# Start addresses of the on-chip tiles: the work region at a multiple of 256 bytes, the raw tiles at a multiple of 64

## What is computed

```
def reference(x, ...):
    x = first_block(x, pre_norm_w, ..., w_out)         # hybrid_layer
    return second_block(x, ln_attn_pre_2, ..., ln_mlp_post_2)

def hybrid_layer(...):
    proj = rms_norm(x, pre_w) @ w_in                   # 1024 -> 6152 columns
    o_sb = merge_heads(stick_breaking_attention(q_sb, k_sb, v_sb)) * silu(sb_gate)      # 8 heads of 64
    o_g  = merge_heads(rms_norm(gated_delta_rule_chunked(...))) * silu(gdn_gate)        # 4 heads of 128
    merged = sigmoid(merge_sb) * (o_sb @ w_branch_sb) + sigmoid(merge_gdn) * (o_g @ w_branch_gdn)
    return x + rms_norm(merged @ w_out, post_w)

def second_block(...):
    x = x + rmsnorm(token_mixer(rmsnorm(x)) @ w_out)   # 4 differential and 8 forgetting heads
    u = square(relu(rmsnorm(x) @ w_up))                # 1024 -> 4096
    return x + rmsnorm(u @ w_down)                     # 4096 -> 1024
```

## The kernel before

| tiles | start, modulo 256 |
|---|---|
| `hT`, `ring`, `raw_ring`, `x1`, `sig_sb`, `consts` | 128 |
| `osb`, `ogd`, `mix`, `merged`, `ring_u`, `u`, `qk`, `b`, `sig_gd`, `rawb`, norm scratch, `wab_s`, `wf_s`, `cin` | 64 |
| `rawg`, `rawsb`, `g`, `s`, `diag`, `q_sq` | 112 |

## Time and profile before

### The profile page before, as it was taken

How to read it: one execution, slowest core, us unless ns; L and a number is a source line. 1 busy time by engine, 2 the same in 40 slices (tenths; PEclk the granted TensorE clock), 3 DMA queues, 4 the chain that set the end, 5 groups by cost and what they waited for, 6 DMA issues and landing times.

```text
span 1102.8 us, 15036 instructions
## 1 busy us (share of the span) xinstructions
PE 1088.4 (99%) x5749; PEld 889.9 (81%) x5749; DVE 537.1 (49%) x1155; ACT 570.2 (52%) x1086; POOL 436.1 (40%) x236
## 2 busy tenths in 40 slices
PE   8999999999999999999999999999999999999997
PEld 7877878778888788888778787789888888888886
DVE  3739789788665224142445455535111115444444
ACT  6556767767678642353465566554222224333333
POOL 4334342442433444543133322344444446444441
PEclk9999999999999999999999999999999999999999
DMA  9133121221322332623222321222333324322212
GB/s 261 48 91 87 48 68 41 76 59 37 97 58 60 93 96 96 229 78 80 77 66 70 97 77 59 77 88 75 107 95 96 96 96 134 105 97 96 97 47 77
DMA packets 140530, 97.24 MB, mean 88 GB/s; under 512 B 9014, under 2 KB 125091, under 8 KB 140459
## 3 DMA queue, kind: packets, MB, share of 16 engines
q1 hardware_dynamic: 138728, 95.03, 29.0%
q10 hardware_dynamic: 1730, 1.25, 0.4%
HBM read 94.14 MB, written 2.91 MB: 88 GB/s over the span
## 4 chain that ended last, share of the span: by engine, by line
PE 95%; ACT 2%; DVE 1%; DMA 1%; issue 0%; POOL 0%; SPq 0%; ACTq 0%; DVEq 0%
PE bank L460 32%; PE bank L1191 14%; PE bank L1173 14%; PE bank L489 6%; PE bank L845 4%; PE bank L871 4%; PE bank L855 4%; PE bank L1204 2%; PE bank L667 1%; PE bank L685 1%; PE bank L610 1%; PE bank L598 1%; PE bank L1019 1%; PE bank L981 1%; PE bank L1001 1%; PE bank L1008 1%
## 5 line engine op out<-in xcount | busy, mean ns | idle before, releaser
L2457 POOL TENSOR_TENSOR ring<-raw_ring,ring 128x1024 fp32r<-128x1024 f32 x160 | 389.7, 2439 | 574.6 <-ACT ring L1217 574.6
L460 PE MATMUL bank<-hT,ring 128*128 128x512 f32 x1536 | 396.0, 403 | 0.5 <-ACT rawsb L1292 0.5
L460 PEld LDWEIGHTS bank<-hT,ring 128*128 128x128 f32 x1536 | 278.0, 189 | 58.3 <-issue 7.5
L1217 ACT CAST ring<-raw_ring 128x1024 fp32r<-128x1024 f32 x160 | 167.3, 1047 | 111.6 <-PE bank L1191 90.2
L1191 PE MATMUL bank<-ring,ring_u 128*128 128x512 f32 x672 | 154.0, 392 | 0.0
L1173 PE MATMUL bank<-hT,ring 128*128 128x512 f32 x672 | 152.5, 390 | 0.0
L1191 PEld LDWEIGHTS bank<-ring,ring_u 128*128 128x128 f32 x672 | 126.4, 188 | 27.4
L1173 PEld LDWEIGHTS bank<-hT,ring 128*128 128x128 f32 x672 | 126.1, 188 | 26.1
L2432 DVE TENSOR_TENSOR ring_u<-u,ring_u 128x1024 fp32r<-128x1024 f32 x32 | 81.2, 2543 | 74.9 <-ACT ring_u L1791 74.9
L2437 DVE TENSOR_TENSOR u<-u 128x512 f32<-128x512 f32 x32 | 22.9, 715 | 139.2 <-ACT u L1798 139.2
L1798 ACT ACTIVATE u<-bank 128x512 f32<-128x512 f32 x32 | 19.1, 598 | 115.4 <-PE bank L1173 108.4
(11 more groups left out here) (292 smaller groups left out, 1482.4 us busy)
## 6 DMA issues: line engine op xcount, KB each, us to landing
raw_ring<-in_w_in SPq DMA_DIRECT2D x144, 256.0 KB, 3.2
raw_ring<-in_w_up SPq DMA_DIRECT2D x64, 256.0 KB, 3.2
raw_ring<-in_w_down SPq DMA_DIRECT2D x64, 256.0 KB, 2.7
raw_ring<-in_w_out SPq DMA_DIRECT2D x32, 256.0 KB, 3.0
x<-in_x SPq DMA_DIRECT2D x8, 512.0 KB, 5.7
raw_ring<-in_w_branch_sb SPq DMA_DIRECT2D x8, 256.0 KB, 2.8
raw_ring<-in_w_branch_gdn SPq DMA_DIRECT2D x8, 256.0 KB, 3.2
cum<-cums SPq DMA_DIRECT2D x4, 512.0 KB, 5.4
```

Source lines behind the costliest of these rows:

```text
L460: p = pe.matmul(bank, m.slab_k8(n % 4)[:, a, k, :], m.hT[:, b, k, :], start=term == 0, stop=term == 23)
L1217: act.copy(m.ring[:, q, 0, :], m.raw_ring[:, q, :]).then_inc(s.slab_hi[q], 1)
L2457: pool.tensor_tensor(m.ring[:, q, 1, :], m.raw_ring[:, q, :], m.ring[:, q, 0, :].bitcast(F32), ALU.subtract).then_inc(s.slab_lo[q], 1)
```

## The change

`r4` is rounded up to a multiple of 256, and inside the first layer's list of tiles the place behind `cin` is rounded up to a multiple of 64. Nothing else differs: each engine has the same instructions in the same order with the same waits.

```
--- before.py
+++ after.py
@@ -118,7 +118,7 @@
         cursor += 11 * 512
         small = cursor
         cursor += 4 * 560 + 768
-        r4 = cursor
+        r4 = -(-cursor // 256) * 256
@@ -183,6 +183,7 @@
         self.ogd = take("ogd", [P, 2, 4, T], F32R)
         raw_a = off[0]
         self.cin = take("cin", [P, 3, T + 4])
+        off[0] = -(-off[0] // 64) * 64
         self.rawg = take("rawg", [P, T])
         self.rawsb = take("rawsb", [P, 4, T])
```

## The result

The changed kernel takes 1107.78 us (median of 7 runs, 1107.65 to 1108.47), the kernel before, timed beside it, 1104.52 us (7 runs, 1104.26 to 1104.89). The ratio is 1.003, with a 95% interval of 1.0021 to 1.004: **slower by 3.3 us**, where 7.9 us less was forecast. The forecast's sign, its time and its range are wrong, and the noise is well under the difference.

A forecast was written before the change was run, and what follows sets the result against it. PE, busy 99% of the span, was taken to bound the kernel. Terms of 3.84 + 1.27 + 0.42 + 1.70 + 0.6 + 0.1 = 7.9 us led from the median of 1104.8 to 1096.9 us, range 1094.0 to 1102.0.

The forecast's parts named there:

- a reading that fits: Large fp32r matmuls: moving operand read from start to end of its last 256-byte block; 213.3 ns for 512 columns at 0.
- The term of L845: L845, 192 matmuls: moving `osb` and `ogd` from 64 to 0 cuts 233.3 to 213.3 ns, 3.84 us less.
- The stationary terms: L855, L871, L1191, L1204: stationary `merged`, `mix`, `ring_u` from 64 to 0 save 1.27, 0.42 and 1.70 us.
- `qk` and `b`: `qk` in L952, L1001, L967, `b` in small float32 matmuls: from 64 to 0, 0.6 and 0.1 us less.
- The rival on the slower side: L845, `merged`, `mix`, `ring_u`: distance between operands decides, growing to 128; 4.7 us more, 1109.5 us; chance 0.06.
- the 120 ns of the half tiles: Matmuls of 256 columns, moving from 128: 1,152 bytes read to the block's end give 120.0 ns; the row has 119.8.
- `merged` carries a rhythm over from L845: L855 and L871: 4.4 of the 6.6 ns are a load-and-matmul rhythm from L845; if only that went, 0.84 us.
- The constant pitch: fp32r matmuls of 512 columns: the skill's 215.8 ns whatever the address; by it L845 would gain 3.4 us, not 3.8.
- no effect: Whole kernel: pitches differ by role or stage, address has no part; 1104.8 us, give or take 0.5; chance 0.09.

The follow-up runs named there:

- the blocks: Kernel of only fp32r matmuls on zeros, the whole computation left out, 28 blocks of 72 with varied start pairs: 226.9, 232.9, 232.2, 229.0 ns at distances 0, 64, 128, 192.
- the blocks in the kernel's order: Matmul-only kernel, computation left out, layouts of `osb` then `merged`, with or without stops: `merged` 22.41 us for 96 without stops, 22.27 us behind one.

## Why the prediction was wrong

**What held.** PE bounds the kernel and a shorter or longer pitch goes through in full. The pitches 226.7, 228.9 and 233.3 ns do depend on addresses. POOL, ACT and DVE have no part: their busy times stayed, and moving the raw tiles by 16 bytes changed nothing.

**The step that failed** is "a reading that fits": that the moving operand is read from its start to the end of its 256-byte block. It was fitted to rows in which the moving operand started at only two places, 128 and 64, and the one row at 64 had another distance to the stationary operand too. At 0 the rule had no row at all. Pairs with both at 0, at 64 and at 128 have one and the same pitch (the blocks, and L1174 at 0 as at 128). The term of L845, 3.84 us, half of the sum, measured 0.01: the pitch stayed at 233.3 ns, where by the prediction's own sign anything over 226.7 refuted it.

**The stationary terms** (`merged`, `mix`, `ring_u`: 1.27 + 0.42 + 1.70 us) took for granted that 0 is as good for the stationary operand as 128. What the rows showed was a distance of 0 against one of 192, and the change made it 128. They measured nothing for `merged`, a loss of 0.40 us in the 90 of L872 with `mix` (and 0.14 in the 33 of L856 ahead of them), and losses of 2.34 and 0.27 us in the two long pieces with `ring_u`. Had all been put at 128, or all at 0, the same three terms with 1.27 for L845 would have come out as written: 4.7 us, measured 4.5 to 4.9.

**`qk` and `b`** (0.6 and 0.1 us): both operands moved together, the distance stayed 0, and the mean of one matmul of `qk` with 512 columns was 391 and is 390 ns. Nothing that can be measured, as a distance that stays 0 would have it; these matmuls were not tried in blocks.

**The rival on the slower side** named the right quantity, gave it 0.06, and had the wrong law. It let the excess grow with the distance and had 240.0 ns for L845 and 231.1 for `ring_u`, 1109.5 us. Measured: 233.3 and 232.4, since at 128 the pitch is no longer than at 64. By its own sign, a pitch of L845 over 233.3 ns, it did not come true either. Two of its counter-arguments were weak. `b` by `b` at 275 ns against 273 was taken as evidence against it, but fp32r matmuls of 128 columns don't see the distance at all (8.27 us a block at all four), so small matmuls may well say nothing on it; plain float32 ones like `b` by `b` were not tried. And "equal remainders would leave the 120 ns of the half tiles unexplained" turned out to be the very point: at 256 columns a distance of 0 is the slow one.

**"`merged` carries a rhythm over from L845"** was right in the main; both the blocks in the kernel's order and the stop in front of it show it. What is carried is the even spacing, not the pitch of L845: behind `osb` with a stop ahead, at the same 233.3 ns, `merged` had 229.2. It should have lowered the confidence: one pair of starts with two pitches can't come from the length of one operand's read alone.

**The constant pitch and the lines of 16 bytes.** No pair of starts came under 226.7 ns for 512 columns; the three pitches of the prediction are 13.3 to 20 ns over 213.3, not 11 to 20 as it says. The Trainium skill (TensorE: Matmul & The Clock Gate, "Back-to-back issue gap") has N / 2.4 + 2.5, that is 215.8 ns, and no term for the address; it calls this the gap of an isolated matmul and has about 131 ns for a stream of loads and matmuls. Neither was reached here. And `r4` moved by 64 bytes shortened the pitch of L845 by 6.7 ns. That speaks against "no effect", which the prediction inferred from the 16-byte lines in the Trainium skill (SBUF — State Buffer, "Specifications (TRN2)"): these lines are not the whole account.

**Still open.** Why the distances rank as they do, and why 256 columns rank otherwise, was measured and not explained. That two streams of reads by PE hinder one another where they meet within 256 bytes is an inference. The 13.3 ns that remain over 213.3 at distance 0 were not taken apart. At distance 128 there are two rhythms as well: 229 and 238 ns in turn (233.3 ns; L846, `merged` and `mix` after the change), and a cycle of seven between 228 and 241 ns (232.4; `ring_u`). Both were seen in blocks behind a stop, so a stop does not select between them, and what does was not found out.

## What to carry to other kernels

Align operands to each other before aligning them to a round number: for fp32r matmuls of 512 columns, let the stationary and the moving tile start at the same remainder modulo 256, itself a multiple of 32, and check all pairs that a tile enters when it is moved. For 256 columns this is no advice: there distance 0 was the slowest of the four. When two addresses explain a pitch equally well, a kernel of blocks with the grid of pairs settles it in one run, and should come before any sum is built on either.

## What the hardware showed that I had not expected

- A fp32r matmul of 512 columns with a new 128 x 128 stationary operand each time has a pitch of 226.7, 233.3, 232.4 and 228.9 ns at distances 0, 64, 128 and 192 in the sixteen blocks, the same at every start that is a multiple of 64, and 3% between best and worst. Behind other stretches, 128 and 192 can also have 233.3 ns.
- With 256 columns it is 120.0 ns at distance 0 and 113.3 at 64 (8.91 and 8.46 us for 72); with 128 columns it is 111.6 ns at all four.
- Rhythms are kept: the same pair of addresses ran at an even 233.3 ns for 186 matmuls in a row, and behind a stop of PE at 228.9 ns, in a cycle of 232, 226 and 229.
- 3.57 us of idle PE were followed by more than 5 us at a granted clock of 0.50. In this kernel, bound by PE, that wait cost its own length and about 3.0 us more, 2.7 of them at the low clock; the better rhythm behind it won back 0.4 us in L855 and as much again in L871.
